# The last two units of the MLA gate grow together, tile by tile over K, in four banks

## The reference, cut to what matters

```
h   = rmsnorm(x, norm_g)
u   = h @ mla_w_in                 # columns: c_q (384) | c_kv (256) | k_rope (32) | z (1024)
c_q  = rmsnorm(c_q,  mla_q_norm)   # 3 tiles of 128 rows in the kernel
c_kv = rmsnorm(c_kv, mla_kv_norm)  # 2 tiles
q        = c_q  @ mla_w_q_b        # 16 heads, 64 + 32 columns each, the 32 are rotated
k_nope,v = c_kv @ mla_w_kv_b       # 16 heads, 64 + 64 columns each
y = attention(q, (k_nope, k_rope), v) * silu(z)
```

## Time and profile before

| what | value |
|---|---|
| runs, median (lowest to highest) | 2151.73 us (2150.18 to 2152.19) |
| the profiled execution | 2151.38 us, of which the span is 2149.6 us |
| mean granted TensorE clock | 0.977 |
| TensorE matmul busy | 2040.2 us, 95% of the span |
| z0 to z7 | about 1405.7 to 1498.3 us after the span's start |
| first matmul of the first head | 1503.11 us |
| first score maxima of MLA | 1518.23 us |

### The profile page before, as it was taken

One profiled execution on the slowest core, in us unless ns is written; L12 is line 12 of the kernel. 1 busy time (PEld: TensorE's weight loads), 2 busy tenths in 40 slices (PEclk: granted clock), 3 DMA queues, 4 the chain that ended last, 5 costly groups with the idle time before them and its releaser, 6 DMA issues.

```text
span 2149.6 us, 26333 instructions
## 1 busy us (share of the span) xinstructions
PE 2040.2 (95%) x9488; PEld 1649.8 (77%) x9488; DVE 1038.6 (48%) x1212; ACT 674.9 (31%) x1083; POOL 1025.3 (48%) x651
## 2 busy tenths in 40 slices
PE   4999999988999999999999999999899999989997
PEld 3777776877888878878887888887677777768785
DVE  6645554636442212212212248332787788864446
ACT  3335554231121000000000024112466666660322
POOL 1545555521743543543453347333555566553364
PEclk9999999997999999999999999999899999999998
DMA  3100000112211111211111123111000000001123
GB/s 140 51 21 21 17 13 20 49 40 88 98 59 49 60 58 49 69 59 49 49 61 49 46 64 112 39 49 41 30 21 20 20 20 20 30 30 49 39 69 117
DMA packets 31660, 106.65 MB, mean 50 GB/s; under 512 B 3458, under 2 KB 3650, under 8 KB 31604
## 3 DMA queue, kind: packets, MB, share of 16 engines
q1 hardware_dynamic: 27520, 96.14, 13.6%
q10 hardware_dynamic: 4084, 9.74, 1.3%
HBM read 101.51 MB, written 4.26 MB: 49 GB/s over the span
## 4 chain that ended last, share of the span: by engine, by line
PE 84%; DVE 7%; ACT 4%; issue 4%; POOL 1%; ACTq 0%; DVEq 0%; DMA 0%; POOLq 0%
PE ps L228 56%; PE ps L374 8%; PE ps L245 3%; PE ps L258 3%; PE ps L618 2%; PE ps L606 2%; PE ps L619 2%; DVE mx L719 1%; PE ps L625 1%; PE ps L605 1%; PE ps L604 1%; ACT mla_p_hi L665 1%; PE ps L650 1%; PE ps L648 1%; DVE S_all L1297 1%
## 5 line engine op out<-in xcount | busy, mean ns | idle before, releaser
L1964 POOL TENSOR_TENSOR w_hi<-w_raw,zero 128x1024 fp32r<-128x1024 f32 (+2 forms) x173 | 320.3, 1851 | 790.8 <-PE ps L228 580.6
L1966 POOL TENSOR_TENSOR w_lo<-w_raw,w_hi 128x1024 fp32r<-128x1024 f32 (+2 forms) x173 | 407.3, 2355 | 13.6
L228 PE MATMUL ps<-h_hi,w_lo 128*128 128x512 f32 x1328 | 335.1, 395 | 5.3 <-DVE x L505 5.1
L228 PE MATMUL ps<-h_hi,w_hi 128*128 128x512 f32 x1328 | 328.0, 389 | 0.0
L228 PE MATMUL ps<-h_lo,w_hi 128*128 128x512 f32 x1216 | 300.6, 389 | 0.0
L228 PEld LDWEIGHTS ps<-h_hi,w_lo 128*128 128x128 f32 x1328 | 249.5, 189 | 60.1 <-issue 9.1
L228 PEld LDWEIGHTS ps<-h_hi,w_hi 128*128 128x128 f32 x1328 | 249.3, 188 | 51.7
L674 POOL TENSOR_TENSOR probs_lo<-probs,mla_p_hi 128x512 fp32r<-128x512 f32 x192 | 191.1, 1015 | 169.0 <-ACT probs L667 167.1
L228 PEld LDWEIGHTS ps<-h_lo,w_hi 128*128 128x128 f32 x1216 | 228.7, 188 | 47.8
L719 DVE TENSOR_REDUCE mx<-ps 128x1 f32<-128x128 f32 (+1 forms) x192 | 141.0, 755 | 79.4 <-PE ps L650 44.3
L674 POOL TENSOR_TENSOR probs_lo<-probs,fox_p_hi 128x512 fp32r<-128x512 f32 (+1 forms) x96 | 95.3, 1010 | 107.8 <-ACT probs L667 107.8
(11 more groups left out here) (351 smaller groups left out, 3675.3 us busy)
## 6 DMA issues: line engine op xcount, KB each, us to landing
w_raw<-in_wpack SPq DMA_DIRECT2D x173, 512.0 KB, 3.3
x<-in_xT ACTq DMA_DIRECT2D x16, 512.0 KB, 8.2
out<-result SPq DMA_DIRECT2D x8, 512.0 KB, 2.9
p_raw<-in_pT ACTq DMA_DIRECT2D x1, 1024.0 KB, 4.9
pos_i<-in_pos SPq DMA_DIRECT2D x1, 512.0 KB, 6.3
const_stage<-in_consts SPq DMA_DIRECT2D x1, 404.0 KB, 3.2
vec<-in_vecs SPq DMA_DIRECT2D x1, 284.0 KB, 5.4
mla_q_hi<-c_neg ACTq DMA_DIRECT2D x16, 4.0 KB
```

The costliest lines, as they stand in the source:

```text
L228: last = nc.tensor.matmul(dst[:, half, :], w[slot][:, kt, :], a[:, i, t], start=(n == 0), stop=(n == total - 1))
L1964: nc.gpsimd.tensor_tensor(w_hi[s][:, kts, :], raw[s][:, kts, :], no_change[:, kts, :], ALU.add).then_inc(w_hi_done, 1)
L1966: nc.gpsimd.tensor_tensor(w_lo[s][:, kts, :], raw[s][:, kts, :], w_hi[s][:, kts, :].bitcast(F32), ALU.subtract)\
```

## The change

z0 to z5 stay as they are, except that `spread_q`, `sum_kv` and `spread_kv` follow z0, z1 and z3 where they followed z1, z3 and z5. z6 and z7 are made together: for each tile of K, six matmuls of z6 and six of z7, z6 in banks 4 and 5, z7 in banks 6 and 7. Both units must be split before the first of them. After each of the first seven tiles of K a semaphore, `h_free`, says that this tile of h is no longer read.

The split inputs are laid out anew so that each needs one tile of h: `cq_hi` on `h_hi` 0 to 2, `ckv_hi` on 3 and 4, the low parts likewise on `h_lo`, and the head buffers on tiles 5 to 7 of each. ACT's high parts wait for `h_free` and no longer for z7, and stand ahead of the Silu of z6 and z7; DVE's low parts stand ahead of the scaling of z6 and z7. ACT's copies of the rotated key wait for z7. TensorE begins the first head without waiting for z6 and z7 to be scaled, and waits for that before the first maxima. FoX, an attention of the first block, gets the same buffer order, at other addresses within its room.

```diff
-            between = {1: spread_q, 3: sum_kv, 5: spread_kv}
-            for i in range(DT):
+            between = {0: spread_q, 1: sum_kv, 3: spread_kv}
+            for i in range(DT - 2):
...
+            NKV.wait(pe, "h", 2)
+            for i in (DT - 2, DT - 1):
+                pe.wait_ge(w_split, U_Z + i + 3)
+            for kt in range(DT):
+                for i in (DT - 2, DT - 1):
+                    for half in range(2):
+                        for n, (w, a) in enumerate(((w_lo, h_hi), (w_hi, h_lo), (w_hi, h_hi))):
+                            last = nc.tensor.matmul(Z_BANKS[i][:, half, :], w[(U_Z + i) % 2][:, kt, :], a[:, kt, cols(half)],
+                                                    start=(kt == 0 and n == 0), stop=(kt == DT - 1 and n == 2))
+                    if kt == DT - 1:
+                        last.then_inc(unit_done, 1)
+                if kt < DT - 1:
+                    last.then_inc(h_free, 1)
...
+            silu(6)
+            silu(7)
...
         def mla_setup_act(act):
             act.wait_ge(kr_step, 4)
+            act.wait_ge(unit_done, U_Z + DT + 2)
...
-            pe.wait_ge(z_read, DT)
+            pe.wait_ge(z_read, DT - 2)
```

More of the change, by code:

```diff
@@ L578, in max_width, with buffers @@
             return w, i // 4 * HALF + w
[L580 to L583, removed]
+        def buffers(k, qk_at, klo_at, vaug_at, vlo_at, phi_at):
+            q_hi = [at(f"{k}_q_hi{b}", qk_at[b], [P, T], F32R) for b in range(2)]
+            q_lo = [at(f"{k}_q_lo{b}", qk_at[b] + 4096, [P, T], F32R) for b in range(2)]
+            k_hi = [at(f"{k}_k_hi{b}", qk_at[b] + 8192, [P, T], F32R) for b in range(2)]
             k_lo = [at(f"{k}_k_lo{b}", klo_at + 4096 * b, [P, T], F32R) for b in range(2)]
@@ L738, in build @@
         fox = Attention("fox", FOX_H, HD, HD + 2, HD + 3, True)
-        fox.bufs, fox.v_lo, fox.p_hi = buffers("fox", R_X, R_X + 24576, R_S + 8192, R_S + 20480, R_S + 24576)
+        fox.bufs, fox.v_lo, fox.p_hi = buffers("fox", (R_X, R_X + 12288), R_X + 24576, R_S + 8192, R_S + 20480, R_S + 24576)
         fox.f_in = [sem(f"fox_f_in{b}") for b in range(2)]
@@ L743, in build @@
         mla = Attention("mla", MLA_H, MASK_ROW0, MASK_ROW0 + N_MASK_ROWS, MASK_ROW0 + N_MASK_ROWS + 1, False)
-        mla.bufs, mla.v_lo, mla.p_hi = buffers("mla", R_H + 40960, R_S + 8192, R_S + 16384, R_S + 24576, R_S + 4096)
+        mla.bufs, mla.v_lo, mla.p_hi = buffers("mla", (R_H + 20480, R_H + 53248), R_S + 8192, R_S + 16384, R_S + 24576, R_S + 4096)
         mla_vT = at("mla_vT", R_W + 16384, [HD, T])
@@ L780, in maxima @@
                         pe.wait_ge(mla_constants, 6)
+                        pe.wait_ge(z_read, DT)
                 for i in MAX_AFTER.get(g, ()):
@@ L1469, in build @@
         k_rope = at("k_rope", R_S + 4096, [P, T])
-        cq_hi, cq_lo = at("cq_hi", R_H, [P, 3, T], F32R), at("cq_lo", R_H + 12288, [P, 3, T], F32R)
-        ckv_hi, ckv_lo = at("ckv_hi", R_H + 24576, [P, 2, T], F32R), at("ckv_lo", R_H + 32768, [P, 2, T], F32R)
+        cq_hi, cq_lo = at("cq_hi", R_H, [P, 3, T], F32R), at("cq_lo", R_H + 32768, [P, 3, T], F32R)
+        ckv_hi, ckv_lo = at("ckv_hi", R_H + 12288, [P, 2, T], F32R), at("ckv_lo", R_H + 45056, [P, 2, T], F32R)
         min_read, kr_step, z_read = sem("min_read"), sem("kr_step"), sem("z_read")
-        z_silu = sem("z_silu")
+        z_silu, h_free = sem("z_silu"), sem("h_free")
+        Z_BANKS = (pjA, pjB) * (DT // 2 - 1) + (PS[:, 4:6, :], PS[:, 6:8, :])
         CR, SR = slice(64, 96), slice(96, 128)
@@ L1544, in z_scaled @@
                 dve.wait_ge(unit_done, U_Z + i + 3)
-                nc.vector.tensor_tensor(mix[:, i, :], flat((pjA, pjB)[i % 2]), rb3[:, :], ALU.mult).then_inc(z_read, 1)
+                nc.vector.tensor_tensor(mix[:, i, :], flat(Z_BANKS[i]), rb3[:, :], ALU.mult).then_inc(z_read, 1)
             norm_diag(dve, NQ)
@@ L1550, in mla_in_dve @@
                 add_squares(NKV, i)
-            z_scaled(1)
             NQ.wait(dve, "bc", 1)
@@ L1554, in mla_in_dve @@
                 norm_scaled(NQ, u5[:, k, :], u5[:, k, :], vec[:, V_QN + k:V_QN + k + 1]).then_inc(NQ["h"], 1)
+            z_scaled(1)
+            norm_diag(dve, NKV)
             z_scaled(2)
             z_scaled(3)
-            norm_diag(dve, NKV)
-            z_scaled(4)
-            z_scaled(5)
             NKV.wait(dve, "bc", 1)
@@ L1562, in mla_in_dve @@
                 norm_scaled(NKV, u5[:, 3 + k, :], u5[:, 3 + k, :], vec[:, V_KVN + k:V_KVN + k + 1]).then_inc(NKV["h"], 1)
-            z_scaled(6)
-            z_scaled(7)
+            z_scaled(4)
+            z_scaled(5)
             for s, n, k0, hi, lo in ((NQ, 3, 0, cq_hi, cq_lo), (NKV, 2, 3, ckv_hi, ckv_lo)):
-                s.wait(dve, "h", n)
                 for k in range(n):
@@ L1569, in mla_in_dve @@
                     nc.vector.tensor_tensor(lo[:, k, :], u5[:, k0 + k, :], hi[:, k, :].bitcast(F32), ALU.subtract).then_inc(s["lo"], 1)
+            z_scaled(6)
+            z_scaled(7)
         def mla_in_act(act):
@@ L1583, in mla_in_act, with silu @@
             square(NKV, 1, 4)
-            for i in range(DT):
-                if i == 4:
+            def silu(i):
+                act.wait_ge(z_read, i + 1)
+                nc.scalar.activation(mix[:, i, :], mix[:, i, :], ACT.Silu).then_inc(z_silu, 1)
+            for i in range(DT - 2):
+                if i == 2:
                     norm_root(act, NKV, KVL, DT)
@@ L1588, in mla_in_act @@
                     act.dma_start(sq[MASK_ROWS, :], mask_rows[:, T:2 * T]).then_inc(mask_in, 16)
-                act.wait_ge(z_read, i + 1)
-                nc.scalar.activation(mix[:, i, :], mix[:, i, :], ACT.Silu).then_inc(z_silu, 1)
-            act.wait_ge(unit_done, U_Z + DT + 2)
+                silu(i)
             for s, n, k0, hi in ((NQ, 3, 0, cq_hi), (NKV, 2, 3, ckv_hi)):
@@ L1595, in mla_in_act @@
                 for k in range(n):
+                    act.wait_ge(h_free, k0 + k + 1)
                     nc.scalar.activation(hi[:, k, :], u5[:, k0 + k, :], ACT.Copy).then_inc(s["hi"], 1)
+            silu(6)
+            silu(7)
         mla.n_lo = 3
```

## The result

The changed kernel takes 2155.06 us in the median of 16 runs (2153.15 to 2157.31), the kernel before 2151.68 us (2149.85 to 2152.91). The ratio is 1.0017, 95% interval 1.0009 to 1.0025: 3.4 us slower. The interval leaves out 1, so the change does cost time, but less than the 0.2% that the prediction took as what can be told from no change. The forecast was +1.9 us and same; the range to 2156.2 holds the time.

The account below looks back on a forecast made before the run. TensorE, busy 95% of the span, was taken as the bound: z7 ending later +4.75 us, the clock +1.3, a shorter tail -4.15, together +1.9 on 2151.38, giving 2153.3 us; range 2149.8 to 2156.2.

Parts of the forecast that it names:

- the split of z7 that loses its cover: Ahead of the pair: POOL splits z7's weights only after z5, 4.37 us, so TensorE's first matmul waits until 1481.17.
- step 1: z5's end: the third L284 group now stands ahead of z5, adding 1.32 and 0.45 us; z5 ends at 1476.62.
- step 4: Clock behind the new gap ahead of the pair: slowed matmuls cost +1.3 us, bounds 0 to 3.0.
- step 10: Rotation and split of the first queries: begin at E + 8.25, last 7.45 us, maxima at E + 15.7, saving 4.15 us.
- the third case: Rival of a slower clock: falls behind both gaps, step 4 costing 3.0, maxima E + 16.6; +4.5 us, 2155.9; 12 in 100.
- Step 8: First head's split is late: first matmul at E + 3.2, queries at E + 7.5, up to 1.5 us later.
- E: The end of z7, from which the prediction counts the times of the tail up to the first maxima.
- Step 7: DVE's two low keys beside POOL's casts: 3.2 to 4.1 us, bounds 2.44 and 4.1; DVE free at E + 7.6 to 8.5.
- Steps 5, 6, 9: Tail: c_q and c_kv parts leave the chain; rotated keys copied by E + 4.3; POOL's constants done by E + 10.5.
- the pair does not wait: Rival: no gap ahead of z6 and z7, z7 ends at 1498.58; -3.95 us, 2147.4; 6 in 100.
- The clock decides, slower: Rival: clock falls behind both gaps, 3.0 us at the pair, queries 1.5 late; +4.5 us, 2155.9; 12 in 100.
- Banks in turn cost the clock: Rival: cycling four banks runs half the pair's 96 matmuls at 0.41 us, +8.9; about 2160.9; 2 in 100.

Follow-up runs that it names:

- e1_catchup: Changed kernel, but z6 does its first four K tiles alone, z7 catches up, the last four alternate; 2148.72 us, 0.9986 against the kernel before.
- e4_warm: Changed kernel with 18 spare matmuls in the gap ahead of the pair, results thrown away; 2151.98 us, 1.0003 against the kernel before.
- e2_lead4: Changed kernel with z6 leading z7 by four K tiles from start to end; 2147.01 us, 0.9981 against the kernel before.
- e6_casts_late: e2_lead4 with ACT's rotated-key copies ahead of the last two Silus and POOL's mask casts held until DVE's low keys are made; 2144.68 us, 0.9965 against before.
- e3_lead8: Changed kernel with z6 whole, then z7 whole, tile by tile over K, no alternation; 2147.54 us, 0.9982 against the kernel before.
- e8_again: The changed kernel, unaltered, run once more for a second trace; 2154.32 us in one run.
- e7_fox_back: Changed kernel with the FoX query and key buffers at their addresses of before; 2156.22 us, 1.0018 against the kernel before.
- e9_lead8_keys: e6_casts_late with z6 whole ahead of z7, as in e3_lead8; 2144.53 us, 0.9966 against the kernel before.

## Why the forecast was right, and what was mis-sized

The step that carried it, the split of z7 that loses its cover, was right in place and price: gap 4.54 us, ended by POOL's `w_lo`, TensorE's first matmul 0.14 us behind it (forecast 0.13). z0's scaling to z5's took 1.77 us longer, as step 1 said. e1_catchup shows that this gap with its clock is what turned the change into a loss: without it the rest of the change gives 3.9 us.

What was off is two sizes, step 4 and step 10, each by 1.0 us, which together are the 2.0 us that the sum missed. So the time lies nearer the third case (+4.5) than the forecast (+1.9), and above 2154.9, where the forecast put the end of its likely times; the upper end of the range, which holds it, was taken from that third case.

- *Step 4, the clock.* Forecast 1.3, inside the bounds of 0 to 3.0. From z0's scaling, z7 ended 7.07 us later than before (88.62 against 81.55), which is 4.75 + 2.3; e4_warm gives 2.2 back. I priced it from a gap behind which eight matmuls ran at 0.50; here it was twelve.
- *Step 8, the first head.* It began 3.17 us behind z7's end (forecast 3.2), but its queries came at E + 9.2: the clock fell again, 18 matmuls in 5.98 us. I had allowed up to E + 9.0, and took E + 8.25 for the rotation.
- *Step 7, low keys.* 4.03 us, near the upper bound of 4.1, with casts beside both. (By its own words, 2.44 and two casts of 1 us, that bound should have been 4.4.) Free at E + 8.5, so the queries decided, 0.77 us behind.
- *Step 10.* Maxima at E + 16.7 where I took 15.7; the third case had 16.6. Together: +4.75 + 2.3 - 3.15 = +3.9, the stretch's +3.92. (The upper bound of 17.0 is not what step 8's E + 9.0 and 7.45 give, 16.45; with the measured E + 9.2 they do give 16.7.)
- *Steps 5, 6, 9.* As forecast: low parts done 5.8 us before z7's end; rotated keys copied at E + 4.3 (1508.20 + 2.00 against 1505.86); POOL's constants in time.

Of the rivals, "the pair does not wait" fell with the first row of the chain. "The clock decides, slower" was half true: both falls came, the second at its full price in the tail, the first at 2.3 and not 3.0, so the sum stayed under 4.3. "Banks in turn cost the clock" fell with e1_catchup and e2_lead4: at clock 1.00 four banks in turn run at the full cadence, 96 matmuls in 21.77 us. The Trainium skill, "TensorE: Matmul & The Clock Gate", section "A second HAM failure mode: psum-queue depth-cycling", tells of a kernel whose clock went to and fro as it cycled through banks; these traces do not show that here.

Step 7's cause is borne out by e6_casts_late, 3.90 us beside POOL's casts against 2.35 without them. The Trainium skill, "SBUF — State Buffer", section "Who interferes with whom", says that a DVE instruction with two SBUF inputs contends with a GpSimd instruction that reads SBUF, for ports that one of them holds at a time; the two lengths agree with it.

Where the expected gain went, then: with the gap gone, the rest of the change took 3.9 to 4.6 us off the path (e1_catchup, e2_lead4, e3_lead8). The early release, the new order of ACT's and DVE's queues and the first head that no longer waits for the scaling were not taken apart. Starting two units at once in a ring of two slots put 7.8 us back on it (e1_catchup against the changed kernel): 7.1 as the gap and the slower pair, and 0.7 in the tail, where the clock did not fall a second time in e1_catchup.

## What to carry to other kernels

Two units that start together need both slots of a two-slot ring, so the split of the second is uncovered at their start, and when they end together so is that of the unit behind them. Let one lead by as many tiles as the split lasts, counting what stretches it (a lead of four tiles, 5.4 us, was 0.8 us too short beside the low parts), or don't pair them: finishing only the last unit K tile by K tile is enough to free its input early. Price a new gap of TensorE with the clock behind it, here half as much again as the gap itself. When a wait is taken off a tail, look next at the order in the queue of the engine that remains: two copies moved ahead of two Silus gave 1.7 us.

## What was not expected of the hardware

A gap of 3.2 us ahead of the first head was followed by a lower clock in four traces (changed, e8_again, e7_fox_back, e4_warm: 18 matmuls in 5.97 to 5.99 us) and not in e1_catchup, where they took 4.2. It did not fall at once: in the changed kernel the first five matmuls behind the gap still came 0.22 to 0.31 us apart and the next eight 0.37 to 0.43. Nor does what ran ahead of the gap tell them apart: in e4_warm that was 22 us at clock 1.00, as in e1_catchup. Why stays open. The window of e1_catchup:

```profile
1500.00:1504.40 4.40, 4.28 (x19) 3.56 (x20) 3.01 (x2) 2.57 (x3) 3.94 (x5) 1.00 0.37 121
```

DVE's low parts with two SBUF inputs and POOL's splits stretch each other, and either can be the one that grows. In e2_lead4 it was the split (above). In e9_lead8_keys the split kept its 2.40 us and the three low parts beside it took 5.32 (e1_catchup, with no split beside them and ACT's copies setting the pace: 3.89):

```profile
1491.33 2.40 POOL L1988 TENSOR_TENSOR w_lo<-w_raw,w_hi 128x1024 fp32r<-128x1024 f32 x1
...
1491.76 5.32 DVE L1582 TENSOR_TENSOR cq_lo<-u,cq_hi 128x1024 fp32r<-128x1024 f32 x3 [12.17 <-ACT cq_hi L1618]
1497.01 2.35 DVE L1582 TENSOR_TENSOR ckv_lo<-u,ckv_hi 128x1024 fp32r<-128x1024 f32 x2
```
